# Later row sums, one root for two norms, a fuller stick-breaking stage, and GpSimd's groups behind the norms' factors

## The reference, cut to what matters

```python
def rms_norm(x, g):
    return x * rsqrt(mean(x * x, -1) + 1e-6) * g

def first_block(x, ...):
    for layer in range(2):
        x = x + 0.5 * swiglu_ffn(x, ffn1_norm[layer], ...)      # norms 1 and 4
        if layer == 0: x = x + retention_dilated_mixer(x, ...)  # norm 2
        else:          x = x + stick_breaking_mixer(x, ...)     # norm 5
        x = x + 0.5 * swiglu_ffn(x, ffn2_norm[layer], ...)      # norms 3 and 6
    return rms_norm(x, final_norm)                              # joined with the next: norm 7

def hybrid_layer(x, mod, ...):                                  # norms 7, 8 and 9, 10
    shift1, scale1, gate1, shift2, scale2, gate2 = split(mod, 6)
    h = rms_norm(x, norm1) * (1 + scale1) + shift1
    x = x + gate1 * (concat(pool_mixer, nsa_mixer)(h @ w_in) @ w_out)
    h2 = rms_norm(x, norm2) * (1 + scale2) + shift2
    return x + gate2 * (square(relu(h2 @ w_ff1)) @ w_ff2)

def second_block(x, c, ...):
    for l in range(2):
        mod = silu(c) @ w_mod[l] + b_mod[l]
        x = hybrid_layer(x, mod, ...)
    return x
```

## Time and profile before

| | |
|---|---|
| time, median of three runs | 3310.84 us (3310.39 to 3319.28) |
| the profiled execution's own time | 3303.49 us |
| its span in the trace | 3301.7 us |
| granted TensorE clock, mean | 0.994 |
| HBM read | 361.92 MB, 110 GB/s over the span |
| first slab's first matmul to the first matmul behind the broadcast, norm 6 and norm 4 | 15.45 us and 24.31 us |

### The profile page before, as it was taken

How to read it: one execution, slowest core, us unless ns; L and a number is a source line. 1 busy time by engine, 2 the same in 40 slices (tenths; PEclk the granted TensorE clock), 3 DMA queues, 4 the chain that set the end, 5 groups by cost and what they waited for, 6 DMA issues and landing times. The chain is left out here.

```text
span 3301.7 us, 40587 instructions
## 1 busy us (share of the span) xinstructions
PE 3241.3 (98%) x15564; PEld 2540.4 (77%) x15564; DVE 1669.3 (51%) x2088; ACT 1143.3 (35%) x1680; POOL 1279.9 (39%) x632
## 2 busy tenths in 40 slices
PE   8999999999999999999899999999999999999999
PEld 6888876688887888887578888665788878478887
DVE  4444446454445445346664444755644456564343
ACT  3223311532233222237652222446322243652231
POOL 4777200067777777740027775030667002000000
PEclk9999999999999999999999999999999999999999
DMA  6554321145544554431135443310444332012222
GB/s 202 152 150 149 117 87 39 52 142 151 151 142 128 153 153 141 152 115 52 42 87 152 146 146 115 83 52 26 140 153 140 102 95 65 26 65 101 89 102 76
DMA packets 334882, 365.68 MB, mean 111 GB/s; under 512 B 31408, under 2 KB 286512, under 8 KB 334512
## 3 DMA queue, kind: packets, MB, share of 16 engines
q1 hardware_dynamic: 309744, 277.98, 27.2%
q0 software_dynamic: 25024, 86.16, 8.2%
HBM read 361.92 MB, written 2.18 MB: 110 GB/s over the span
## 5 line engine op out<-in xcount | busy, mean ns | idle before, releaser
L325 ACT CAST w_hi<-raw 128x2048 fp32r<-128x2048 f32 x247 | 471.4, 1908 | 1163.1 <-PE ps L376 936.7
L376 PE MATMUL ps<-h_hi,w_hi 128*128 128x512 f32 x2064 | 808.9, 392 | 4.7 <-DVE xT L2376 2.5
L376 PE MATMUL ps<-h_hi,w_lo 128*128 128x512 f32 x2064 | 804.0, 390 | 0.0
L376 PE MATMUL ps<-h_lo,w_hi 128*128 128x512 f32 x2064 | 803.7, 389 | 0.0
L329 DVE TENSOR_TENSOR w_lo<-raw,w_hi 128x2048 fp32r<-128x2048 f32 x247 | 605.4, 2451 | 266.8 <-ACT w_hi L325 266.1
L689 PE MATMUL ps<-a_hi,w_hi 128*128 128x512 f32 x1344 | 523.7, 390 | 0.4
L689 PE MATMUL ps<-a_lo,w_hi 128*128 128x512 f32 x1344 | 522.9, 389 | 0.0
L689 PE MATMUL ps<-a_hi,w_lo 128*128 128x512 f32 x1344 | 522.9, 389 | 0.0
L376 PEld LDWEIGHTS ps<-h_hi,w_hi 128*128 128x128 f32 x2064 | 387.8, 188 | 88.5 <-issue 9.1
L376 PEld LDWEIGHTS ps<-h_hi,w_lo 128*128 128x128 f32 x2064 | 387.8, 188 | 81.6
L376 PEld LDWEIGHTS ps<-h_lo,w_hi 128*128 128x128 f32 x2064 | 388.0, 188 | 80.5 <-issue 1.2
(11 more groups left out here) (354 smaller groups left out, 4071.5 us busy)
## 6 DMA issues: line engine op xcount, KB each, us to landing
raw<-in_ffn_w_in SPq DMA_DIRECT2D x174, 512.0 KB, 5.1
raw<-in_w_ff SPq DMA_DIRECT2D x128, 512.0 KB, 4.1
m_in<-in_w_mod POOLq DMA_DIRECT2D x96, 512.0 KB, 4.2
raw<-in_ffn_w_out SPq DMA_DIRECT2D x88, 512.0 KB, 4.2
m_in<-in_w_ff POOLq DMA_DIRECT2D x64, 512.0 KB, 4.0
raw<-in_hyb_w_in SPq DMA_DIRECT2D x28, 512.0 KB, 4.6
raw<-in_w_in SPq DMA_DIRECT2D x28, 512.0 KB, 4.7
raw<-in_sb_w_in SPq DMA_DIRECT2D x24, 512.0 KB, 4.3
```

Source lines behind the costliest of these rows:

```text
L325: eng.copy(w_hi[:, e % 2], raw[:, e % 2]).then_inc(s["w_hi_done"], 1)
L376: mm = pe.matmul(ps[:, bank], wbuf[a][:, e % 2, at:at + P], hbuf[b][:, k], start=(k == 0 and n == 0), stop=(k == KC - 1 and n == 2))
```

## The change

Five edits. (a) **Stick stage**: half 1 fills 12 products a step over steps 4 to 11 for what it filled with 8 over steps 4 to 15, and 12 a step over steps 12 to 15 with a third slab of w_out (`pe_out_more`, with `om_part`, a hi and lo copy of two finished output chunks, and `out_more` on VectorE for the eight evacuations); the outp phase behind it has one slab for two (`pe_outp_stick`). The splits of operands and slabs move to steps 7 to 14. (b) **Deferred norms**: sums behind chunk 7 for 6, fold behind k=2 of the next slab's first piece, broadcast behind its k=6. (c) **Norm 7**: one root of the product of both means, (m0 + eps) * eps + m1 in place of the square and the second factor, 7 links for 15 to r_both, whose broadcast stands behind chunk 5; the lone first factor is computed behind it. (d) **Rewritten slab**: its first chunk waits for one h_lo, not two. (e) **GpSimd**: g=4 waits for the third factor in place of 16 x_ready, g=8 (which waited for nothing) for the fourth; the wait ahead of ff_bias(0, 1..3) is one for the sixth factor and stands ahead of slab_bias, which was ahead of the wait; ff_bias(1, 1..3) wait for the eighth factor in place of the ninth norm's h_lo. `bias_done` is waited for at 1, not 2.

```diff
@@ -174,7 +174,7 @@
-phases.append(("outp", A["sb_w_out"][0], 4, 2, ("one",), "stick"))
+phases.append(("outp", A["sb_w_out"][0], 6, 1, ("one",), "stick"))
...
@@ -375,8 +376,8 @@
-if k == 2 and soon:
-    soon()
+if soon and k in soon:
+    soon[k]()
@@ -444,7 +445,7 @@
-pe.wait_ge(s["h_lo_done"], KC * (c.hnorms - 1) + max(i, 1) + 1)
+pe.wait_ge(s["h_lo_done"], KC * (c.hnorms - 1) + (i if c.rewrite else max(i, 1)) + 1)
@@ -467,8 +468,8 @@
-elif i == 6:
-    pe_bcast(pe, c, r_both, 1, 15)
+elif i == 5:
+    pe_bcast(pe, c, r_both, 1, 7)
@@ -481,15 +482,10 @@
-    elif c.deferred and not first and i == 6:
+    elif c.deferred and not first and i == 7:
-    elif c.deferred and not first and i == 7:
-        pe_fold(pe, c, 0, 1)
-if first:
-    c.soon = lambda: pe_fold(pe, c, 0, 1)
-    c.mid = lambda: pe_bcast(pe, c)
-elif c.deferred:
-    c.soon = lambda: pe_bcast(pe, c)
+if c.deferred:
+    c.soon = {2: lambda: pe_fold(pe, c, 0, 1), 6: lambda: pe_bcast(pe, c)}
@@ -504,7 +500,7 @@
-pe_bcast(pe, c, rcol, 3, 0)
+pe_bcast(pe, c, rcol, 3, 6)
@@ -651,6 +647,25 @@
+def pe_out_more(pe, c):
+    pe.wait_ge(s["w_lo_done"], c.slab + 1)
+    pe.wait_ge(s["om_lo"], 2)
+    pe.wait_ge(s["oq_x"], c.oq)
+    wbuf = (w_hi, w_lo)
+    for d in range(KC):
+        if d:
+            pe.wait_ge(s["om_x"], d)
+        for k in range(2):
+            at = k * D + d * P
+            for m, (a, b) in enumerate(THREE):
+                mm = pe.matmul(ps[:, 7], wbuf[a][:, c.slab % 2, at:at + P], om_part(k, b),
+                               start=(k == 0 and m == 0), stop=(k == 1 and m == 2))
+                if k == 1 and m == 2:
+                    mm.then_inc(s["slab_used" if d == KC - 1 else "om_mm"], 1)
+                    c.slab += d == KC - 1
+                yield
@@ -679,6 +694,28 @@
+def pe_outp_stick(pe, c, products):
+    pe.wait_ge(s["w_lo_done"], c.slab + 1)
+    pe.wait_ge(s["y6_lo"], 1)
+    pe.wait_ge(s["x_ready"], KC * c.outs)
+    pe.wait_ge(s["sb_exp"], 2 * c.sb - 2)
+    pe.wait_ge(s["om_x"], KC)
+    for d in (2, 3, 4, 5, 7):
+        products(0, 0, d, True, False)
+    pe.wait_ge(s["sb_exp"], 2 * c.sb)
+    pe.wait_ge(s["sb_y"], 8)
+    for d in (0, 1, 6):
+        products(0, 0, d, True, False)
+    pe.wait_ge(s["a_lo_done"], c.outp + 1)
+    c.order = update_order(c)
+    for d in c.order:
+        mm = products(0, 1, d, False, True)
+        mm.then_inc(s["slab_used" if d == c.order[-1] else "bank_done"], 1)
+    c.slab += 1
+    c.outp += 1
+    c.outs += 1
...
@@ -806,7 +848,8 @@
-a_split(eng, c, 1, 1)
+a_split(eng, c)
+split(eng, s0 + 1, s0 - 1)
...
@@ -1183,6 +1227,9 @@
+if ph[0] == "stick":
+    load(1, lambda dst, j: [(dst[:, a * D:(a + 1) * D],
+                             w_out.rearrange("(k p) n -> k p n", p=P)[4 + a]) for a in range(2)])
...
@@ -1333,7 +1384,11 @@
-    return [d for d in range(KC) if divmod(3 * d + 2, 2) == (step - 4, 1 if after_b else 0)]
+    return [step - 4] if after_b and 4 <= step < 12 else []
+def om_ended(step, after_b):
+    return [2 * (step - 12) + after_b] if 12 <= step < 16 else []
...
@@ -1629,15 +1684,19 @@
+elif v >= 12:
+    advance(out_more, 6)
-    advance(out_half, 4)
+    advance(out_half, 6)
+elif v >= 12:
+    advance(out_more, 6)
-    advance(out_half, 4)
+    advance(out_half, 6)
@@ -1793,12 +1852,13 @@
+if ph[3] is not None:
+    eng.wait_ge(s["norm_chain"], c.chain + 2)
+    eng.activation(small[:, 52:56], small[:, 48:52], ACT.Sqrt).then_inc(s["rms_done"], 1)
+    c.chain += 7
-if ph[3] is not None:
-    eng.wait_ge(s["norm_chain"], c.chain + 9)
-    eng.activation(small[:, 52:56], small[:, 48:52], ACT.Sqrt).then_inc(s["rms_done"], 1)
-c.chain += 6 if ph[3] is None else 15
+c.chain += 6
...
@@ -1964,7 +2024,7 @@
-eng.wait_ge(s["bias_done"], 2)
+eng.wait_ge(s["bias_done"], 1)
@@ -1983,17 +2043,20 @@
-        for b in range(2):
-            for d in oq_ended(v, b):
-                if d == 3:
-                    split_hi(eng, s0 + 2, s0)
+        if v == 7:
+            split_hi(eng, s0 + 2, s0)
+        if v == 9:
+            eng.wait_ge(s["sb_y"], 6)
+            for k in range(2):
+                eng.copy(om_part(k, 0), act[:, 12 + k]).then_inc(s["om_hi"], 1)
-            eng.wait_ge(s["sb_y"], 6)
-            a_split_hi(eng, c, 0, 0)
+            split_hi(eng, s0 + 3, s0 + 1)
+        if v == 13:
+            eng.wait_ge(s["sb_y"], 7)
+            eng.copy(a_hi[:, c.outp % 2, 0:SEQ], act[:, 14]).then_inc(s["y6_hi"], 1)
-    split_hi(eng, s0 + 3, s0 + 1)
-c.slab += 2 if half else 6
+c.slab += 3 if half else 6
@@ -2107,8 +2170,8 @@
-if g == 4:
-    eng.wait_ge(s["x_ready"], 2 * KC)
+if g in (4, 8):
+    eng.wait_ge(s["rstd_done"], 2 + g // 4)
@@ -2150,8 +2213,8 @@
+eng.wait_ge(s["rstd_done"], 6)
-eng.wait_ge(s["x_ready"], KC * 5)
@@ -2189,7 +2252,7 @@
-eng.wait_ge(s["h_lo_done"], KC * 9)
+eng.wait_ge(s["rstd_done"], 8)
...
@@ -2270,17 +2332,18 @@
-factor(ps[:, 0, 0:TB], rcol[:, :])
+link(eng, eng.tensor_scalar(ms, ps[:, 0, 0:TB], EPS, None, ALU.add), "norm_chain")
+factor(rcol[:, :])
-factor(means[:, 0], rcol[:, :])
-link(eng, eng.tensor_tensor(ss, rcol[:, :], rcol[:, :], ALU.mult), "norm_chain")
-link(eng, eng.tensor_tensor(ss, ss, means[:, 1], ALU.mult), "norm_chain")
-factor(ss, r_both)
-link(eng, eng.tensor_tensor(r_both, r_both, rcol[:, :], ALU.mult), "norm_chain")
+link(eng, eng.tensor_scalar(ss, means[:, 0], EPS, EPS, ALU.add, ALU.mult), "norm_chain")
+link(eng, eng.tensor_tensor(ms, ss, means[:, 1], ALU.add), "norm_chain")
+factor(r_both)
+link(eng, eng.tensor_scalar(ms, means[:, 0], EPS, None, ALU.add), "norm_chain")
+factor(rcol[:, :])
...
@@ -2548,12 +2619,17 @@
-for d in oq_ended(v, 0):
-    out_part(d)
+for d in om_ended(v, 0):
+    out_more(d)
+if half:
+    for d in oq_ended(v, 1):
+        out_part(d)
+    for d in om_ended(v, 1):
+        out_more(d)
@@ -2572,19 +2648,23 @@
-        for d in oq_ended(v, 1):
-            out_part(d)
-        for b in range(2):
-            for d in oq_ended(v, b):
-                if d == 3:
-                    split_lo(eng, s0 + 2, s0)
+        if v == 7:
+            split_lo(eng, s0 + 2, s0)
+        if v == 10:
+            for k in range(2):
+                eng.wait_ge(s["om_hi"], k + 1)
+                eng.tensor_tensor(om_part(k, 1), act[:, 12 + k], om_part(k, 0).bitcast(F32), ALU.subtract
+                                  ).then_inc(s["om_lo"], 1)
-            eng.wait_ge(s["sb_y"], 6)
-            a_split_lo(eng, c, 0, 0)
+            split_lo(eng, s0 + 3, s0 + 1)
+        if v == 14:
+            eng.wait_ge(s["y6_hi"], 1)
+            r = c.outp % 2
+            eng.tensor_tensor(a_lo[:, r, 0:SEQ], act[:, 14], a_hi[:, r, 0:SEQ].bitcast(F32), ALU.subtract
+                              ).then_inc(s["y6_lo"], 1)
-    split_lo(eng, s0 + 3, s0 + 1)
-c.slab += 2 if half else 6
+c.slab += 3 if half else 6
...
```

More of the change, by code:

```diff
@@ L206, in slabs_of @@
         return {"proj": lambda: len(ph[2]), "outp": lambda: ph[3], "projT": lambda: len(ph[2]),
-                "projV": lambda: len(ph[2]), "projG": lambda: 1, "nsa": lambda: 3, "dilated": lambda: 3, "stick": lambda: 6 if ph[1] == 0 else 2,
+                "projV": lambda: len(ph[2]), "projG": lambda: 1, "nsa": lambda: 3, "dilated": lambda: 3, "stick": lambda: 6 if ph[1] == 0 else 3,
                 "retention": lambda: len(ph[2])}.get(ph[0], lambda: 0)()
@@ L234, in hybrid_stack_kernel @@
         h_lo = sb("h_lo", [P, KC, SEQ], F32R)
+        om_y = sb("om_y", [P, 4, SEQ], F32R, at=place[0])
         act = sb("act", [P, FF_CHUNKS, SEQ])
@@ L696, in begin @@
                 pe.wait_ge(s["a_lo_done"], j + (r0 + 1))
+            if after == "stick":
+                pe_outp_stick(pe, c, products)
+                return
             begin(0)
@@ L706, in pe_outp @@
                 pe.wait_ge(s["att_pt"], 2 * c.att)
-            elif after == "stick":
-                last_banks = (0, 1, 6)
-                pe.wait_ge(s["sb_exp"], 2 * c.sb - 2)
-                pe.wait_ge(s["oq_x"], c.oq)
             else:
@@ L722, in pe_outp @@
                 pe.wait_ge(s["att_w"], c.attg)
-            elif after == "stick":
-                pe.wait_ge(s["sb_exp"], 2 * c.sb)
-                pe.wait_ge(s["sb_y"], 8)
             for d in last_banks:
@@ L789, in a_split_hi, with last_y_hi, last_y_lo @@
             eng.copy(a_hi[:, (c.outp + e) % 2].rearrange("p (a t) -> p a t", a=2), src).then_inc(s["a_hi_done"], 1)
+        def last_y_hi(eng, c):
+            eng.copy(a_hi[:, c.outp % 2, SEQ:], act[:, 15]).then_inc(s["a_hi_done"], 1)
+        def last_y_lo(eng, c):
+            eng.wait_ge(s["a_hi_done"], c.outp + 1)
+            r = c.outp % 2
+            eng.tensor_tensor(a_lo[:, r, SEQ:], act[:, 15], a_hi[:, r, SEQ:].bitcast(F32), ALU.subtract
+                              ).then_inc(s["a_lo_done"], 1)
         def a_split_lo(eng, c, j, e, ahead=0):
@@ L821, in beside_outp @@
             if not last:
-                step(full, full, True, False)
+                if n > 1:
```

(17 more changed lines are left out.)

5 lines of the change are left out of this document (3 added, 2 removed).

## The result

The changed kernel takes 3320.31 us in the median of seven runs (3316.25 to 3325.2), the kernel before 3305.98 in seven of its own (3303.45 to 3319.28, with the three shown above among them). The ratio is 1.0037, with a 95% interval of 1.0025 to 1.0049: slower by 12 us (the two medians lie 14.3 apart). The profiled execution lasted 3320.15 us, its span is 3318.4, so 16.7 us more than the one of before, whose 3303.49 lay at the quick end of its runs. The forecast was 3314, 3.5 us slower; the measured time lies in the range of 3297 to 3324, at the upper end.

A forecast was written before the change was run, and what follows sets the result against it. TensorE, computing for 98% of the span, was taken to bound the kernel. Terms of -10.9 us, plus 14.4 for GpSimd's work moved onto norms 5 and 7, gave +3.5: 3310.84 + 3.5 = 3314 us, range 3297 to 3324.

The forecast's parts named there:

- Norm 1: At norm 1 the broadcast comes 3 products earlier: -0.7 us, or 0 if its third slab waits on w_lo alone.
- Later sums: At norms 2 to 6, 8 and 10 the factor comes 2.8 us later, delaying third slabs: +9.8 us (0 to 20).
- GpSimd off norms 4 and 8: Groups waiting for later factors leave both norms: -8.9 us at norm 4, -2.2 at norm 8, together -11.1.
- Stick stage: outp loses 48 products (-10.9 us), half 1's steps grow 0.28 us each (+3.4): -7.5 us (-10.5 to +0.4).
- One root: At norms 7 and 9: norm 7's shorter chain brings the joint factor sooner, -1.4 us; norm 9 gains 0.
- Norm 5: GpSimd's feed-forward bias (0,0) now runs across norm 5: +6 us (0 to 9); nobody waits for its result.
- Norm 7: GpSimd's bias (1,0) now covers norm 7's updates, chain and rewrite, slowing VectorE: +8.4 us (+2 to +15).
- A: Rival, faster: GpSimd's groups moved onto norms 5 and 7 cost nothing; 3300 us, chance 0.26.
- B: Rival, slower: five operations of norm 7's rewrite each wait for a whole GpSimd instruction; 3324 us, chance 0.10.
- C: Rival, slower: stick stage keeps its pauses and pays in full, +11.3 us for 3.4; 3322 us, chance 0.12.

The follow-up runs named there:

- experiment 9: experiment 5 with the fold behind k=1 and the broadcast behind k=4 of the next slab, not 2 and 6; 3290.32 us, ratio 0.9940.
- experiment 5: The whole change, but with GpSimd's groups kept off every norm from the third on; 3299.14 us, ratio 0.9982 to the kernel before.
- experiment 7: Kernel before with fuller stick stage, GpSimd's groups kept clear of norms, single root and earlier first chunk of the rewritten slab, old sums; 3285.62 us, ratio 0.9940.
- experiment 2: Kernel before with only GpSimd's new waits; 3315.78 us, ratio 1.0030.
- experiment 4: Kernel before with only the fuller stick stage; 3300.42 us, ratio 0.9991.

## Why the prediction was right or wrong

The sign was right, and so were the places of the gains and losses but for norm 9. The size, +3.5 us for +12, was short by some 9. I had given slower by over 0.3% a chance of 0.21 only, and the measured 0.37% lies there (its interval begins at 0.25%). That the time is within the range is partly luck: the forecast was added to 3310.84, and all seven runs of the kernel before have a median of 3305.98. Counted from there the range would have ended at 3319, under the measured 3320.31. By stretches, each from a norm's first slab to the next norm's, the forecast's terms and the two traces (us) are:

| stretch | forecast | trace |
|---|---|---|
| to norm 2 | -0.7 | -1.8 |
| norms 2 and 3 | +2.3 | +2.3 |
| norm 4 | -7.1 | -6.9 |
| norm 5 and the stick stage | -1.0 | +5.4 |
| norm 6 | +1.6 | +1.8 |
| norm 7 | +7.0 | +8.2 |
| norm 8 | -0.4 | +1.0 |
| norm 9 | 0 | +4.8 |
| norm 10 | +1.8 | +2.0 |

Most of the miss sits in two places, norm 5 and norm 9, and in both a good part of it is the clock. Step by step:

1. **Norm 1** (-0.7): the third slab's wait falls from 1.57 to 0.89 us, -0.7 as foretold. The other 1.1 us by norm 2 lie ahead of norm 1's first slab (0.7) and in the clock.
2. **Later sums** (+9.8, of which 9.0 at norms 3, 4, 6, 8 and 10): the five waits of the changed kernel sum to 8.5, and experiment 9 shows their cause. In the trace of the changed kernel the term came out as said. The price by time, alone and under clear groups, is 13.5. Some 3.4 of it are the clock: in the trace of experiment 5 it fell once at norm 3 and once at norm 4, close behind those waits (1.7 us each), in that of experiment 7 at neither. Another 1.1 is the longer wait of experiment 5 at norm 4 (2.70 us for 1.62). The term was a sum of pauses and had no price for what follows them.
3. **GpSimd off norms 4 and 8** (-11.1): norm 4 fell to a clean one, as said. Norm 8 did too, but its stretch in experiment 2 is only 1.1 shorter, not 2.2.
4. **Stick stage** (-7.5): each step grew by 0.26 us, 0.28 was said. But I had filled only pauses, and nearly half of what was absorbed is the clock, which I hadn't looked at. By the medians the stage gave 5.7, and the interval doesn't exclude nothing.
5. **One root** (-1.4): 0 to -4 by the times; norm 7 clean takes 33.98 for 35.34, so -1.4.
6. **Norm 5** (+6): this is where the size failed. I took norm 4's 8.9 less 3, because the later sums would absorb what VectorE loses. They absorbed next to nothing: 6.3 us of pauses for norm 4's 6.5. And the 8.9 was itself a low reading of the clock. In norm 4 of the kernel before, the stretch around the pause had one fall, 1.7 us:

```profile
1054.00:1060.00 6.00, 4.07 (x12) 2.10 (x13) 4.07 (x2) 0.59 (x1) 5.66 (x3) 0.72 0.36 102
```

   In norm 5 three falls cost 5.1. Norm 4 can do the same: in experiment 4, where its code and GpSimd's groups are those of before, it takes 26.75 us for 24.31, with 6.2 of pauses and three falls:

```profile
1054.80:1065.10 10.30, 9.48 (x26) 6.62 (x27) 5.64 (x6) 0.79 (x2) 4.77 (x1) 0.50 0.36 102
```

   That is 11.3 above the clean 15.45, the same as norm 5's 11.3. The term lies above its upper bound of 9.
7. **Norm 7** (+8.4): the changed kernel takes 9.6 us more than the clean one of experiment 5 there, 3.4 of it clock and some 6.4 pauses. So the 8.4 were met by less pause than forecast and a clock that the term didn't have. The rewrite's operations lost 1.14, 2.11, 0.86 and 2.02 us, 6.1 together, for the 6 foretold, though on four operations, not ten; and the rewrite began 1.7 us late behind one small link, where the chain's share was put at 1.4.

Not foreseen at all were 4.8 us between norms 9 and 10, where GpSimd is idle. The trace has them as three falls of the clock more (the first below), with no pause of TensorE above 1.4 us ahead of them, and about the same pauses as before. Experiment 2, whose code at norm 9 is that of the kernel before, lost 3.2 there as well, so it doesn't take edit (d).

```profile
2746.80:2750.40 3.60, 3.60 (x21) 2.87 (x19) 2.61 (x6) 0.00 (x0) 0.00 (x0) 0.53 0.02 7
```

What decides where the clock falls there stays open. It also moves one and the same kernel: the changed one's quickest run (3316.25) had a mean clock of 0.993, its slowest (3325.2) 0.991.

The rivals: A (the moved groups cost nothing) is ruled out by experiments 2 and 5. B foresaw 3324 by whole-instruction waits in the rewrite; the measured time lies nearer to it than to the forecast, but its mechanism is only half true. Two of the rewrite's operations waited so, not five, and its sign, over 25 us from factor to third slab, isn't met by 23.3. Norm 5 cost 11.3, more than B's 9. The Trainium skill, page "SBUF — State Buffer", section "SBUF: two separate sides", has the lock held for the whole instruction of either engine. The traces agree for GpSimd's additions (2.43 us, ending 0.55 behind it) and differ for its scalings, where the same operation lost 0.8 us at the start and nothing in the second half, under an instruction of 2.85. For those the measurement decides. C (the stage pays in full, 6.5 us a step) is ruled out by the measured 5.93. One thing in step 6 was read wrongly in the code without harm: VectorE waits for ff_bias(0, 0) already at the start of the stick stage, at 1480, not far inside it; GpSimd's part of the group was done by 1452.

## What to carry to other kernels

When work of a side engine is moved off a critical stretch, write down the new start and end of every group queued behind it and lay them over all later critical stretches: here each group left norm 4 only to land on norms 5 and 7. A pause of TensorE near a norm can cost more than itself, so price it with the granted clock of stretches that had such a pause, and from more than one trace: the same norm 4 lost 1.7 us to the clock in one and 5.1 in another. Where a fuller stage leaves fewer pauses, look for the clock's gain too. A wait placed inside a group of eight pieces, rather than ahead of it, let two of the groups lie around a norm.
